# Mixer-gate columns moved from the opening loads into the input layer, and raised-layer products without shift columns in the low part

## What is computed

```python
# first block: Fourier + recurrent mixer, then expert-choice MoE (16 experts, width 2816)
mod = silu(c) @ w_ada[0] + b_ada          # 6 x 1024 columns: sh1, sc1, gt1, sh2, sc2, gt2
h   = modulate(rms_norm(x, g_mix), sh1, sc1); proj = h @ w_in[0]   # 3072 columns, also for ctx
x   = x + gt1 * (concat(fourier_mix(u_l), rec_l) @ w_out)
x   = x + gt2 * ec_moe(modulate(rms_norm(x, g_ffn), sh2, sc2), ...)
x   = rms_norm(x, g_final)
# second block: MoBA attention + spatial gating, then relu^2 feed-forward (4096)
h = rmsnorm(x, g_mix_2) * (1 + scale1) + shift1;  proj = h @ w_in_2      # 4608 columns
x = x + gate1 * (merged @ w_out_2);  h = rmsnorm(x, g_ffn_2) * (1 + scale2) + shift2
x = x + gate2 * (square(relu(h @ w_ff1)) @ w_ff2)
# third block, twice: dilated attention + short convolution
h = rms_norm(x, pre_norm_g) * (1 + scale) + shift;  proj = h @ w_in_3[l]  # 4096 columns
x = x + gate * rms_norm(mix @ w_out_3[l], post_norm_g)
```

## Time and profile before

| | us |
|---|---|
| median of 3 runs | 2260.46 (2253.43 to 2266.82) |
| profiled execution, its own time | 2262.27 |
| its span, first to last instruction | 2260.0 |
| PE busy | 1825.0 |
| DVE busy | 787.2 |
| ACT busy | 525.6 |
| mean granted TensorE clock | 0.784 of full speed |

### The profile page before, as it was taken

How to read it: one execution, slowest core, us unless ns; L and a number is a source line. 1 busy time by engine, 2 the same in 40 slices (tenths; PEclk the granted TensorE clock), 3 DMA queues, 4 the chain that set the end, 5 groups by cost and what they waited for, 6 DMA issues and landing times.

```text
span 2260.0 us, 34009 instructions
## 1 busy us (share of the span) xinstructions
PE 1825.0 (81%) x14916; PEld 1152.0 (51%) x14916; DVE 787.2 (35%) x1228; ACT 525.6 (23%) x857; POOL 52.3 (2%) x85
## 2 busy tenths in 40 slices
PE   5999997777777777677676777767899999999897
PEld 3996752212212222221221222221798999998896
DVE  5656630000000000000000000010775788788777
ACT  2430220000000000000000000000574565365664
POOL 0014000000000000000000000000000000000000
PEclk8999987657757655765765665675999999999999
DMA  9867899999999999999999999999744559853541
GB/s 383 299 229 288 345 393 424 425 425 425 425 426 425 425 426 425 425 426 426 425 425 426 426 425 426 425 425 424 254 146 143 169 164 345 285 172 126 168 131 66
DMA packets 159893, 760.64 MB, mean 337 GB/s; under 512 B 10263, under 2 KB 99095, under 8 KB 108216
## 3 DMA queue, kind: packets, MB, share of 16 engines
q1 hardware_dynamic: 156136, 754.07, 83.6%
q10 hardware_dynamic: 3664, 5.24, 0.7%
HBM read 756.13 MB, written 3.14 MB: 336 GB/s over the span
## 4 chain that ended last, share of the span: by engine, by line
DMA 51%; PE 40%; DVE 6%; ACT 1%; issue 1%; SPq 0%; DVEq 0%; ACTq 0%
DMA arena<-in_w_exp_up 22%; DMA arena<-in_w_exp_gate 22%; PE ps L752 19%; PE ps L1160 4%; DMA ring<-in_w_exp_down 3%; PE ps L1018 3%; PE ps L703 3%; PE ps L1032 2%; DMA ring<-in_w_exp_up 2%; PE ps L653 1%; PE ps L896 1%; DVE ring_lo L1607 1%; PE ps L1142 1%; DVE const L1981 1%; DMA ring<-in_w_in 1%; PE ps L746 1%
## 5 line engine op out<-in xcount | busy, mean ns | idle before, releaser
L1018 PE MATMUL ps<-arena,const 128*32 128x352 f32 x2816 | 407.8, 724 | 163.8 <-DMA arena<-in_w_exp_gate 101.3
L1018 PEld LDWEIGHTS ps<-arena,const 128*32 128x32 f32 x2816 | 99.1, 148 | 460.2 <-DMA arena<-in_w_exp_gate 181.6
L1607 DVE TENSOR_TENSOR ring_lo<-ring,w_hi 128x1024 fp32r<-128x1024 f32 x220 | 267.3, 1218 | 74.0 <-ACT w_hi L1208 73.0
L752 PE MATMUL ps<-u_hi,w_hi 128*128 128x258 f32 x960 | 275.5, 287 | 1.2 <-DVE ring_lo L1607 1.1
L1979 DVE TENSOR_TENSOR tail<-tail,ps 128x704 f32<-128x704 f32 x15 | 13.3, 887 | 743.1 <-PE ps L1018 743.1
L752 PE MATMUL ps<-u_hi,ring_lo 128*128 128x258 f32 x960 | 271.2, 282 | 0.0
L752 PE MATMUL ps<-u_lo,w_hi 128*128 128x258 f32 x960 | 271.0, 282 | 0.0
L1208 ACT ACTIVATE w_hi<-ring 128x1024 fp32r<-128x1024 f32 x220 | 230.2, 1050 | 73.7 <-PE ps L1160 30.5
L1018 PE MATMUL ps<-ring,const 128*32 128x352 f32 x1024 | 159.4, 773 | 49.2 <-DMA ring<-in_w_exp_up 36.7
L752 PEld LDWEIGHTS ps<-u_hi,w_hi 128*128 128x128 f32 x960 | 181.6, 189 | 7.3 <-issue 5.2
L752 PEld LDWEIGHTS ps<-u_lo,w_hi 128*128 128x128 f32 x960 | 181.6, 189 | 0.0
(11 more groups left out here) (279 smaller groups left out, 2358.4 us busy)
## 6 DMA issues: line engine op xcount, KB each, us to landing
arena<-in_w_exp_gate SPq DMA_DIRECT2D x96, 1408.0 KB, 35.3
arena<-in_w_exp_up SPq DMA_DIRECT2D x80, 1408.0 KB, 36.5
ring<-in_w_exp_down SPq DMA_DIRECT2D x64, 1536.0 KB, 38.1
ring<-in_w_exp_up SPq DMA_DIRECT2D x48, 1408.0 KB, 35.3
ring<-in_w_in SPq DMA_DIRECT2D x37, 1536.0 KB, 7.0
ring<-in_w_ada SPq DMA_DIRECT2D x32, 1536.0 KB, 9.5
arena<-in_w_exp_down SPq DMA_DIRECT2D x32, 1536.0 KB, 35.4
ring<-in_w_ff SPq DMA_DIRECT2D x18, 1536.0 KB, 7.3
```

What stands on the lines that cost most here:

```text
L752: m = pe.matmul(ps[:, bank, 0:a.shape[-1]], w, a, start=(k == 0 and j == 0), stop=(k == KD - 1 and j == 2))
L1018: m = pe.matmul(ps[32 * j:32 * j + 32, 2 * (k // 8) + i, 0:FJ // 2], XCUR[:, k % 8, :], SLOT[s][:, at:at + FJ // 2], start=(k % 8 == 0), s ...
L1607: tt(slot(c["u"], KD, c["w"], of=ring_lo)[:, :, at], slot(c["u"], KD, c["w"])[:, :, at], w_hi[:, s % HI, :, :].bitcast(F32), ALU.subtract) ...
```

## The change

Two parts.

1. The opening loads only columns 0 to 2047 of `w_ada[0]` (1 MB for each of eight blocks). `first_unit` takes the place of `ada_unit(0, ...)` with four matmuls of 512 columns for eight of 384, `first_turn` does four small matmuls for six. The gate's 1024 columns become eight more thirds (c = 3) that DVE accumulates at items 8, 9, 10, 11, 14, 17, 20, 23 into a fourth `ACC1`; `gate_sum` on PE after item 26 sums it over partitions straight into columns, and DVE adds the bias at item 27. The last step of the normalisation of ctx (x inverse root) leaves the opening and goes, two chunks at a time, into items 0 to 3 of DVE's loop.
2. In the raised layers column T of `U_HI` holds the high part of the shift and column T+1 its low part. `U_LO` goes without the two columns, and the products are ordered high x high, high x low input (256 columns), low weight x high. DVE scales only 256 columns and adds the two shift columns (with the factor 0.125 for queries) in a second instruction with one column.

```diff
+ADA_FIRST = 2048
+THIRD_AT = sorted([(3 + n, n % THIRDS, n // THIRDS) for n in range(THIRDS * KD)] +
+                  [(i, THIRDS, k) for k, i in enumerate((8, 9, 10, 11, 14, 17, 20, 23))])
+GATE_AT = 26
...
-                while third_at[0] < THIRDS * KD and third_at[0] - len(THIRD1) + THIRD_ITEM <= item:
+                while third_at[0] < len(THIRD_AT) and (third_at[0] < len(THIRD1) or
+                                                       THIRD_AT[third_at[0] - len(THIRD1)][0] <= item):
...
+            def first_unit(kc):
+
+                u = ada[0][kc]
+                unit_ready(u)
+                for j in range(CG):
+                    m = pe.matmul(ps[32 * j:32 * j + 32, 6, :], conds[:, kc, :], slot(u, CG, 512)[:, j, :],
+                                  start=(kc == 0), stop=(kc == KD - 1), skip_group_check=True)
+                count(m, "unit_used")
...
+            def gate_sum():
+
+                pe.wait_ge(S("brow_out"), 1)
+                pe.wait_ge(S("first_used"), 1 + max(n for n, (_, c, _) in enumerate(THIRD_AT) if c == THIRDS))
+                for q in range(KD):
+                    m = pe.matmul(ps[:, 5, q:q + 1], ACC1[THIRDS][:, P * q:P * q + P], ones[:, 0:1],
+                                  start=True, stop=True, skip_group_check=True)
+                count(m, "gate_summed")
...
+                if x_hi.shape[-1] > x_lo.shape[-1]:
+                    return (hi, x_hi), (hi, x_lo), (lo, x_hi)
                 return (hi, x_hi), (lo, x_hi), (hi, x_lo)
...
-            rows_out(0)
+            name, n = plan.used[ada[0][KD - 1]]
+            act.wait_ge(S(name), n)
+            mark(act.activation(ROWS0, ps[:, 6, :], ACT.Copy), "rows_out")
...
-                link(dve.tensor_copy(shx[:, :, 0:1], shift.unsqueeze(2)))
-                link(ts(shx[:, :, 1:2], shift.unsqueeze(2), 0.125, None, ALU.mult))
-                link(dve.tensor_copy(U_HI[:, :, T:UCOL], shx))
-                link(tt(U_LO[:, :, T:UCOL], shx, U_HI[:, :, T:UCOL].bitcast(F32), ALU.subtract))
+                link(dve.tensor_copy(U_HI[:, :, T:T + 1], shift.unsqueeze(2)))
+                link(tt(U_HI[:, :, T + 1:UCOL], shift.unsqueeze(2), U_HI[:, :, T:T + 1].bitcast(F32), ALU.subtract))
...
-                mark(tt(TMP[:, it["b"] % 3, :], ps[:, it["bank"], 0:UCOL], R, ALU.mult), "row_scaled")
+                a, b = TMP[:, it["b"] % 3, :], ps[:, it["bank"], :]
+                mark(tt(a[:, 0:T], b[:, 0:T], R, ALU.mult), "row_scaled")
+                mark(ts(a[:, T:T + 1], b[:, T:T + 1], b[:, T + 1:UCOL], scale, ALU.add, ALU.mult), "row_scaled")
...
-            normalise(CTX, CTX)
+            normalise(CTX, CTX, chunks=False)
...
                     for c in chunks:
+                        link(tt(CTX[:, c, :], CTX[:, c, :], rs[:, 0:T], ALU.mult), "normed")
+                    for c in chunks:
                         modulate_chunk(1, c)
```

More of the change, by code:

```diff
@@ L656, in ada_unit, with first_turn, ada_sum @@
                 count(m, "unit_used")
-            def ada_sum(p, acc, by):
+            def first_unit(kc):
[5 more added lines that the diff above has]
+                count(m, "unit_used")
+            def first_turn():
+                pe.wait_ge(S("rows_out"), 1)
+                pick = ident.rearrange("p (j c) -> p j c", j=CG)[:, :, 0:4]
+                for q in range(4):
+                    m = pe.matmul(ps[:, 4, 16 * q:16 * q + 16], ROWS0[:, P * q:P * q + P], pick,
+                                  start=True, stop=True, skip_group_check=True)
+                count(m, "turned")
+            def gate_sum():
[3 more added lines that the diff above has]
+                    m = pe.matmul(ps[:, 5, q:q + 1], ACC1[THIRDS][:, P * q:P * q + P], ones[:, 0:1],
+                                  start=True, stop=True, skip_group_check=True)
+                count(m, "gate_summed")
+            def ada_sum(p, acc, by, n):
                 pe.wait_ge(S("rows_out"), p)
-                pe.wait_ge(S(by), THIRDS * KD)
+                pe.wait_ge(S(by), n)
                 for i in range(2):
@@ L795, in each @@
                         column_sums(two)
-                return dense_blocks(units, lambda it: (U_HI, U_LO), raise_input(), ready="u_split", each=each)
+                return dense_blocks(units, lambda it: (U_HI, U_LO[:, :, 0:T]), raise_input(), ready="u_split", each=each)
             norms = [0]
@@ L1616, in square, with normalise @@
                 link(tt(SQ[:, c, :], src[:, c, :], src[:, c, :], ALU.mult), "squared")
-            def normalise(src, dst=XN, then=lambda c: None):
+            def normalise(src, dst=XN, then=lambda c: None, chunks=True):
                 norms[0] += 1
@@ L1629, in normalise @@
                 link(dve.reciprocal(r, r))
-                for c in range(KD + 2):
+                for c in range(KD + 2 if chunks else 0):
                     if c < KD:
@@ L1693, in mark, with add_to @@
                 ins.then_inc(S(name), 1)
-            def add_to(a, third, k, c, name, n, buffers):
+            def add_to(a, third, k, c, name, n, buffers, before):
                 waits(f"{name}_in{n % buffers}", 16 * (n // buffers + 1))
@@ L1700, in add_to @@
                 else:
-                    waits(name + "_used", n - THIRDS + 1)
+                    waits(name + "_used", before[0])
                     mark(stt(a, third, conds[:, k, c:c + 1], a, ALU.mult, ALU.add), name + "_used")
@@ L1849, in _ @@
                         low_modulated(c, HC, C_HI, C_LO)
[L1850 to L1853, removed]
+                for n, (at, c, k) in enumerate(THIRD_AT):
+                    if at == i:
+                        prior = [m + 1 for m, (_, d, j) in enumerate(THIRD_AT) if d == c and j == k - 1]
+                        add_to(ACC1[c], THIRD1[n % len(THIRD1)], k, 0, "first", n, len(THIRD1), prior)
+                if i == GATE_AT + 1:
+                    waits("gate_summed", 1)
+                    link(tt(mod[:, 0, 16:24], ps[:, 5, 0:KD], V("b_ada", 16, KD), ALU.add))
             waits("evacuated", in1[-1]["items"][-1]["b"] + 1)
```

53 lines of the change are left out of this document (29 added, 24 removed).

## The result

| us | before | after |
|---|---|---|
| median of 20 runs each | 2260.65 (2253.43 to 2268.73) | 2272.26 (2261.84 to 2275.77) |
| profiled execution, its own time | 2262.27 | 2269.41 |
| its span | 2260.0 | 2267.1 |
| PE busy | 1825.0 | 1839.8 |
| DVE busy | 787.2 | 812.1 |

The ratio is 1.0044, with an interval of 1.0034 to 1.0054, thus 7.7 to 12.2 us. The forecast was 2259.7 with a range of 2251 to 2267; the result lies outside it, on the slow side.

A forecast was written before the change was run, and what follows sets the result against it. The experts' weight stream bounds the middle; earlier steps shift its start, and behind it PE's products are mostly the chain. Part 1 at -1.6 and part 2 at +0.8 us took 2260.46 to 2259.7, range 2251 to 2267.

The forecast's parts named there:

- Part 2: Raised layers: narrower products, one-column DVE operation and fewer shift operations, together +0.8 us.
- The order of the three products costs nothing: their waits all stand before the item: Raised layers: reordering each item's three products on PE costs no time, 0 us.
- Opening, -6.0: Opening: with less modulation data queued ahead, the first input-layer weight unit lands at 38.4 instead of 44.4 us, -6.0 us.
- Moved normalisation, +2.7: Input layer's ACT and DVE loop: ctx's normalisation multiplications lengthen the chain in items 1 to 3, +2.7 us.
- Gate on DVE, 0: Input layer: eight more multiply-adds on DVE fit its slack, 0 us; 10.2 us if uncovered.
- its loads, 0: Input layer: the gate's 4.19 MB of loads are absorbed by the queue, 0 us; 5.6 us if uncovered.
- The rival: Turned items: DVE waits for late thirds, low parts come late and PE stands, up to 10.2 us; chance 10%.
- Gate's sum, +1.7: End of the input layer: eight small products on PE sum the gate, +1.7 us.
- 258 to 256 columns, -0.4: Raised layers: a third of the products lose two columns, -0.4 us, with 0 to -7.4 kept as bounds.
- One-column operation, +1.5: Raised layers: DVE's extra instruction counts only at nine scalings in the chain behind the stream, +1.5 us.
- DVE as the bound, the rival on the slow side: Raised layers: the one-column operation costs its length in every item, +22.4 us for the +1.5; chance 5%.

The follow-up runs named there:

- b_shift: Kernel before with `shx` placed behind `arena`, so `arena` lies 64 bytes lower, no instruction changed: 2270.15 us, ratio 1.0037 to before.
- p2_order: `p2_pad` with the three products back in the old order: 2261.91 us in one execution.
- p2_pad: Kernel before with only the raised-layer part of the change, `shx` kept unused so tiles stay at their old addresses: 2267.68 us, ratio 1.0025 to before.
- a_pad64: Changed kernel plus an unused tile of 64 bytes per partition, so `arena` lies where it did before the change: 2265.82 us, ratio 1.002 to before.
- the second execution: A further profiled execution of each kernel, both unchanged: 2266.26 us for after, 2256.45 for before.
- p1_norm_first: `p1_pad` with ctx's normalisation kept in the opening and thirds allowed to issue three items further ahead: 2255.61 us, ratio 0.9973 to before.
- p2_oneop: `p2_pad` with one 257-column row scaling for the two operations, leaving out the shift's low part and query scale: 2267.13 us in one execution.
- b_p128: Kernel before with `arena` 128 bytes higher, at byte 105392: 2269.11 us in one execution.
- p1_pad: Kernel before with only the opening, gate and normalisation part of the change, all tiles at their old addresses: 2261.17 us, ratio 0.9995 to before.

## Why the prediction was wrong

**What failed: "Part 2" had no term for where the tiles lie.** The forecast named the shift's operations, but not that the tile `shx` goes, and that all placed behind it moves. Moving `arena` by 64 bytes alone is worth +8.4 us (`b_shift`), more than any term of the sum. In the stages it is +4.2 us in in1 and +3.6 in ff2, which the sum had at nothing. The rows had a hint: ff2 at 2.721 us an item beside 2.882 in the output layer, for the same form. The prediction says that the rows contain steps in pace, and uses them only as a possible gain of up to 7.4 us for the raised layers. The question to ask was what keeps ff2 and in1 at the fast pace, and whether the change leaves it.

**"The order of the three products costs nothing: their waits all stand before the item" failed.** The waits are as I said. The pace of ff2 isn't: +2.8 us (`p2_order` against `p2_pad`, and `a_pad64` has the slower pace too). Why isn't known. It doesn't add to the placement, since ff2 takes 94.3 us with both, 94.3 with the placement alone and 93.4 with the order alone.

**Opening, -6.0.** Measured -8.7 (44.42 to 35.67) and -8.1 in the second execution. The squared sum of ctx ended 1.9 us sooner, so the issue came at 28.93 for my 30.8, and the load took 6.72 us for 7.6. At my 373 GB/s its 1.57 MB are 4.2 us, so 2.5 us are start-up, for the 3.4 that I took from rows 4. The trace has the queue idle for most of the first microsecond (a share of 0.01 from 28.9 to 30.0 us), then at 202 GB/s for two and at 391. The Trainium skill (DMA: Bandwidth & Descriptors, Anatomy of one DMA) puts the fixed part at about 2.0 us, in a section on DMAs that GpSimd issues, while SP issues these. With my 373 GB/s that would be an estimate of 6.2 us for the measured 6.72, nearer than the 7.6 from my row.

**Moved normalisation, +2.7.** Right: the loop took 2.2 us more in the first pair of executions and 3.2 in the second. Putting it back in `p1_norm_first` takes 2.9 us from the loop, and its removal from the opening is worth nothing, as the sum had it (35.7 us with it and without).

**Gate on DVE, 0, and its loads, 0.** The compute is free. The loads aren't: that the second stretch takes up the 5.6 us holds only if DVE may wait, and it waited 23.9 us. In after this costs nothing that shows, and PE is slower there than it was; with the old pace it costs 4.6 us, most of it through the clock. The rival had 10% and up to 10.2 us, but another way: PE was to stand for late low parts, and it stood for the gate's sum, a wait that the sum of terms doesn't have. **Gate's sum, +1.7**: 1.68.

**258 to 256 columns, -0.4.** In ff1 27 items took 77.67 us for 78.02 at the old place, -0.35, over 132 items -1.7 us; at the new place 78.01, nothing. The bound of -7.4 us was far off. The Trainium skill (VectorE: DVE Perf Modes, The TRN2 errata) has a matmul at 6 cycles plus its columns, by which one of 256 columns would be 109.2 ns at 2.4 GHz. Neither in1 nor ff2 runs at that in any kernel here: they have 113.3 to 120.0 ns at a full clock, and what separates their paces is larger than the two columns.

**One-column operation, +1.5.** 214 ns for 170, and 1.1 us (`p2_pad` against before) to 1.5 (against `p2_oneop`) in the third block alone. DVE as the bound, the rival on the slow side, didn't come.

**Adding up**, after against before, by the table: -8.7 opening, +2.2 loop, +1.7 gate's sum, +4.3 pace of in1, -0.8 experts, +1.4 for in2 to ff1 (-0.1 to -0.2 in the second pair), +3.6 ff2, +3.4 third block, in all +7.1, the difference of the spans. Of the last term the operation is 1.1 to 1.5 and the placement alone 0.3 (`b_shift`); the other 1.6 to 2.0 us occur only where part 2 and the new place come together (`a_pad64`, at the old place, has 294.9), and weren't taken apart. The medians differ by 11.6 us and the second pair of executions by 9.8; the profiled execution of after is one of its faster ones (14 of 20 runs lie at 2271.76 or above), and what the others lose more wasn't profiled.

**Open:** what sets the pace. It isn't the byte alone (`p2_oneop`), it doesn't return after 128 bytes (`b_p128`), and a change in other layers' product order moves ff2. A rival that no run here tests is the place of the instructions themselves, which any edit can move. Not tried: moving the weights' tiles (`w_hi`, `ring_lo`) against the inputs, and adding idle instructions to one engine with all tiles in place. Part 1 as in `p1_norm_first` together with part 2 in the old order wasn't run either; `p2_order` gives no reason to add part 2.

## What to carry to other kernels

A deleted or resized tile is an edit to everything that is placed behind it: list the offsets of the matmul operands before and after, and test a layout change by itself, with a pad that restores them. Such a test is one program against another, so take more than one place and more than one kernel at each. Where the same form of product shows two paces in one trace with PE busy and the clock full, treat the fast one as something that the change can lose, with a price (here 4 to 6% of each such stage), not only as something to win. When one engine becomes slower, it can hide that another is late; the cost comes back when the first is repaired.

## What the runs showed of the hardware

- Back-to-back products of one form (128x128 weights, 256 columns, full clock, no gap) take 113.3, 117.8 or 120.0 ns in in1 and 113.4, 117.8, 118.3 or 118.7 in ff2. The pace was the same in both executions of before and of after, differs by layer, and was another after a move of the work area by 16 or 64 bytes (ratios 1.0035 and 1.0037), in ff2 after a new order of the products in other layers (76.17 to 79.14 us), and in in1 after an edit to instructions that run 1.4 ms later (`p2_oneop`, 48.96 to 50.87 us).
- Gaps of 0.9 and 1.9 us in dense products (`p1_pad`, `a_pad64`) were followed by 20 us at a mean granted clock of 0.83, 6.8 of them at the 1.2 GHz level; one of 1.5 us in `p1_norm_first` wasn't (1.00).
- A DVE operation of one column with its input and its scalar in PSUM takes 214 ns, one of two columns in SBUF 169.
- A load of 1.57 MB on an empty queue landed in 6.72 us; behind three modulation blocks the same load took 13.15. One of 1 MB took 6.2, so size alone doesn't give the time.
